# Stick-breaking scores of a hybrid decoder block: three products of rounded and low parts of q and k in place of one plain fp32 product

## The reference

```python
q = rms_norm(heads(sb_q, SB_HEADS), sb_q_norm_g)
k = rms_norm(heads(sb_k, SB_HEADS), sb_k_norm_g)
...
z = jnp.einsum("bhqd,bhkd->bhqk", q_blk, k).astype(jnp.float32) * scale
visible = (kpos[None, :] < t[:, None]) & key_valid[None, :]
log_beta = jax.nn.log_sigmoid(z)
log_one_minus = jnp.where(visible, jax.nn.log_sigmoid(-z), 0.0)
log_remaining = lax.cumsum(log_one_minus, axis=3, reverse=True) - log_one_minus
a = jnp.where(visible, jnp.exp(log_beta + log_remaining), 0.0)
return jnp.einsum("bhqk,bhkd->bhqd", a.astype(v.dtype), v)
```

## Time and profile before

| | |
|---|---|
| three runs, median (lowest to highest) | 1952.8 us (1946.82 to 1953.89) |
| the profiled execution, its own time | 1955.42 us |
| its span, first to last instruction | 1953.6 us |
| mean granted TensorE clock | 0.977 of full |
| TensorE matmul busy | 1859.0 us (95%) |
| VectorE, ScalarE, GpSimd busy | 1392.0, 836.3, 616.0 us |

### The profile page before, as it was taken

How to read it: one execution, slowest core, us unless ns; L and a number is a source line. 1 busy time by engine, 2 the same in 40 slices (tenths; PEclk the granted TensorE clock), 3 DMA queues, 4 the chain that set the end, 5 groups by cost and what they waited for, 6 DMA issues and landing times.

```text
span 1953.6 us, 30169 instructions
## 1 busy us (share of the span) xinstructions
PE 1859.0 (95%) x11211; PEld 1686.9 (86%) x11211; DVE 1392.0 (71%) x2885; ACT 836.3 (43%) x1429; POOL 616.0 (32%) x639
## 2 busy tenths in 40 slices
PE   7899999898986999999999999999999999999999
PEld 7776676666654778899999999999999999999999
DVE  5455455565552654389988869999778888888887
ACT  4335445454453542233434456666433333333332
POOL 4024032041140100059888832121212232223221
PEclk9999989999986999999999999999999999999999
DMA  3220211201203632259999978998889999999996
GB/s 122 99 70 22 71 55 44 82 33 45 87 6 121 199 125 81 84 175 348 334 322 325 326 234 318 336 339 319 282 271 333 336 331 341 333 336 342 331 333 228
DMA packets 150961, 416.12 MB, mean 213 GB/s; under 512 B 16000, under 2 KB 64288, under 8 KB 148768
## 3 DMA queue, kind: packets, MB, share of 16 engines
q1 hardware_dynamic: 110784, 269.31, 38.9%
q0 software_dynamic: 40032, 144.89, 22.7%
HBM read 364.55 MB, written 49.58 MB: 212 GB/s over the span
## 4 chain that ended last, share of the span: by engine, by line
PE 65%; issue 1%; DMA 1%; POOL 1%; DVE 1%; ACT 0%; SPq 0%; DVEq 0%; POOLq 0%; ACTq 0%
PE psE L84 21%; PE psE L86 21%; PE psE L85 21%; PE psE L2093 1%; PE psE L2094 1%; PE psE L2054 1%; DMA gates<-mix_gates 0%; DMA mixer_out<-mixed_heads 0%; POOL few_gathered L1660 0%; POOL expert_lo L1666 0%; DVE few_y L1896 0%; DVE expert_lo L1702 0%; SPq L1514 0%; PE psE L2113 0%; PE psE L2060 0%
## 5 line engine op out<-in xcount | busy, mean ns | idle before, releaser
L84 PE MATMUL psE<-x2h,expert_hi 128*128 128x384 f32 x1024 | 347.3, 339 | 3.8 <-POOL expert_lo L1666 3.8
L84 PE MATMUL psE<-w_hi,expert_hi 128*128 128x384 f32 x1024 | 343.3, 335 | 2.0 <-DVE expert_lo L1702 2.0
L86 PE MATMUL psE<-x2h,expert_lo 128*128 128x384 f32 x1024 | 342.9, 335 | 0.0
L85 PE MATMUL psE<-x2l,expert_hi 128*128 128x384 f32 x1024 | 342.8, 335 | 0.0
L85 PE MATMUL psE<-w_lo,expert_hi 128*128 128x384 f32 x1024 | 342.8, 335 | 0.0
L86 PE MATMUL psE<-w_hi,expert_lo 128*128 128x384 f32 x1024 | 342.7, 335 | 0.0
L1547 ACT ACTIVATE expert_hi<-raw 128x1024 fp32r<-128x1024 f32 x288 | 303.5, 1054 | 63.3 <-PE psE L86 53.6
L1702 DVE TENSOR_TENSOR expert_lo<-raw,expert_hi 128x1024 fp32r<-128x1024 f32 x214 | 261.9, 1225 | 84.7 <-ACT expert_hi L1547 83.1
L1660 POOL DMA_INDIRECT few_gathered<-in_peer_v,picked_expert x128 | 142.3, 1112 | 398.9 <-DVE few_y L1896 356.9
L1666 POOL TENSOR_TENSOR expert_lo<-raw,expert_hi 128x1024 fp32r<-128x1024 f32 x74 | 177.7, 2402 | 161.2 <-ACT expert_hi L1547 159.8
L1601 ACT ACTIVATE w_hi<-gelu 128x384 fp32r<-128x384 f32 x128 | 67.4, 527 | 344.8 <-PE psE L86 342.3
(11 more groups left out here) (339 smaller groups left out, 3518.4 us busy)
## 6 DMA issues: line engine op xcount, KB each, us to landing
raw<-in_peer_u SPq DMA_DIRECT2D x128, 512.0 KB
raw<-in_peer_v SPq DMA_DIRECT2D x128, 512.0 KB
expert_acts<-gelu SPq DMA_DIRECT2D x124, 192.0 KB
gelu<-expert_acts SPq DMA_DIRECT2D x124, 192.0 KB
expert_gates<-shared SPq DMA_DIRECT2D x16, 1024.0 KB, 10.6
gates_in<-expert_gates SPq DMA_DIRECT2D x32, 512.0 KB
ring<-in_w_xonly SPq DMA_DIRECT2D x24, 512.0 KB, 3.3
ring<-in_w_full SPq DMA_DIRECT2D x16, 512.0 KB, 3.8
```

The lines of the kernel that those rows point to most:

```text
L84: nc.tensor.matmul(out, sh, mh, start=first, stop=False)
L85: nc.tensor.matmul(out, sh, ml, start=False, stop=False)
L86: return nc.tensor.matmul(out, sl, mh, start=False, stop=last)
```

## The change

q and k, scaled in place as before by VectorE, are each split: ScalarE copies them to fp32r (the high part of q lies where `exp_g_row` was, that of k in the third row of `conv_act`), and VectorE subtracts that from the fp32 value and writes the low part in place. The copies stand on ScalarE behind the rounding of the next weight chunk (the filler's `kk` place) and the filler place "inverse0", the subtractions on VectorE behind the nine block copies. The score becomes three products, high by high, high of k by low of q, low of k by high of q, summed in PSUM, and the first score of a pair waits for both low parts.

```diff
--- before.py
+++ after.py
@@ -238,8 +238,8 @@
         x, xl = in_place("x", "xl", [P, DC, TOK])
         ring_h = sb("ring_h", [P, FRONT_RING, DC, P], F32R)
         ring, ring_l = in_place("ring", "ring_l", [P, FRONT_RING, DC, P])
-        proj = sb("proj", [P, 4, TOK])
-        qz = sb("qz", [P, 2, SEQ])
+        proj, proj_r = in_place("proj", "proj_low", [P, 4, TOK])
+        qz, qz_r = in_place("qz", "qz_low", [P, 2, SEQ])
         v = sb("v", [P, NT + 1, SEQ])
         ba = sb("ba", [P, NT + 1, 16])
         soft, floor = sb("soft", [P, NT + 1, 16]), sb("floor", [P, NT + 1, 16])
@@ -274,10 +274,12 @@
         soft_h = act_r[:, :, :].rearrange("p w t -> p (w t)")[:, 0:2 * SEQ].rearrange("p (s t) -> p s t", t=SEQ)
         acc_h = kq_r[:, :, :, :].rearrange("p n w t -> p (n w t)")[:, 0:2 * SEQ].rearrange("p (s t) -> p s t", t=SEQ)
         qd = sb("q_decayed", [P, NT + 1, P])
-        egr = sb("exp_g_row", [P, NT + 1, P])
+        egr, egr_r = in_place("exp_g_row", "q_high", [P, NT + 1, P])
         kbg, ktl, vb = (sb(name, [P, NT + 1, P]) for name in ("kbg", "k_tail", "v_beta"))
         rows_all, rows_r = in_place("rows_all", "soft_lo", [P, 2, 2, TOK])
         lows = rows_r[:, :, :, :].rearrange("p k e t -> p (k e t)")[:, 0:4 * SEQ].rearrange("p (s t) -> p s t", t=SEQ)
+        qn_h, qn_l = egr_r[:, :, :].rearrange("p n t -> p (n t)")[:, 0:SEQ], qz_r[:, 0, :]
+        kn_h, kn_l = act_r[:, 2, :], proj_r[:, 0, :]
         soft_l, acc_l = lows[:, 0:2, :], lows[:, 2:4, :]
         row_heads = sb("row_heads", [P, 2, P])
         decays = sb("decays", [P, NT + 1, 2, 2, P])
@@ -303,7 +305,7 @@
             first_level qd_ready level_ready xt_ready x_transposed x_ready y_ready y_copied x_products x_updated wt_ready
             wt_copied v_new_ready v_new_copied o_ready state_product state_ready o_copied o_squared o_sum o_log o_root
             z_ready z_scores z_ln z_soft soft_split later_summed later_high later_ready cumulated att_exp att_out masks_ready
-            att_stored pair_done o_normed o_final state_blank att_inputs state_decayed""".split()
+            att_stored pair_done o_normed o_final state_blank att_scaled att_high att_inputs state_decayed""".split()
         S = {name: sem(name) for name in names}
         x_loaded = [sem(f"x_loaded{k}") for k in range(DC)]
         v_loaded = [sem(f"v_loaded{k}") for k in range(DC)]
@@ -327,7 +329,7 @@
                    wt_copied=1, v_new_ready=5, v_new_copied=5, o_ready=1, state_product=4, state_ready=4, o_copied=1,
                    o_squared=1, o_sum=1, o_log=1, o_root=1, z_ready=1, z_scores=10, z_ln=10, z_soft=10,
                    soft_split=10, later_summed=8, later_high=8, later_ready=8, cumulated=10, att_exp=10, att_out=1, att_stored=1,
-                   o_normed=1, o_final=1, state_blank=1, att_inputs=1, state_decayed=1)
+                   o_normed=1, o_final=1, state_blank=1, att_scaled=2, att_high=2, att_inputs=2, state_decayed=1)
         inc = lambda ins, name, by=1: ins.then_inc(S[name], by)
 
         def waiter(eng, i):
@@ -655,6 +657,11 @@
                         turned = bank[:, y_bank(n), 0:2 * P].rearrange("p (e b c) -> p e b c", e=2, b=2)
                     inc(nc.scalar.activation(into, turned, ACT.Copy), "x_ready")
                 split("inverse0")
+                for part, (high, scaled) in enumerate(((qn_h, qn), (kn_h, kn))):
+                    wait("att_scaled", part + 1)
+                    wait("qd_ready", 1)
+                    wait("transposed", 1)
+                    inc(nc.scalar.activation(high, scaled, ACT.Copy), "att_high")
                 for u, (unit, a) in enumerate(UNITS):
                     if unit == "level":
                         for n in range(NT + 1):
@@ -944,14 +951,18 @@
                                                     xt[0:r, n - 1, :, 0:r], ALU.subtract), "xt_ready")
                 dve.wait_ge(S["w_taken"], CHUNKS.index(("q", i)) + 1)
                 wait("roots", 4)
-                nc.vector.scalar_tensor_tensor(out=qn, in0=qn, scalar=gq, in1=rt[:, 2, META:], op0=ALU.mult,
-                                               op1=ALU.mult)
+                inc(nc.vector.scalar_tensor_tensor(out=qn, in0=qn, scalar=gq, in1=rt[:, 2, META:], op0=ALU.mult,
+                                                   op1=ALU.mult), "att_scaled")
                 inc(nc.vector.scalar_tensor_tensor(out=kn, in0=kn, scalar=gk, in1=rt[:, 3, :], op0=ALU.mult,
-                                                   op1=ALU.mult), "att_inputs")
+                                                   op1=ALU.mult), "att_scaled")
                 for n in range(NT + 1):
                     for rows in halves if n else [slice(0, META)]:
                         last = nc.vector.tensor_copy(mtc[rows, n, :, 0:rows.stop - rows.start], mtat[rows, n, :, 0, rows])
                     inc(last, "blocks_ready")
+                for part, (low, scaled, high) in enumerate(((qn_l, qn, qn_h), (kn_l, kn, kn_h))):
+                    wait("att_scaled", part + 1)
+                    wait("att_high", part + 1)
+                    inc(nc.vector.tensor_tensor(low, scaled, high.bitcast(F32), ALU.subtract), "att_inputs")
                 at("inverse0")
                 for u, (unit, a) in enumerate(UNITS):
                     if unit == "products":
@@ -1225,13 +1236,14 @@
                         r, q0 = tile_rows(kb), first_query(kb)
                         lo, hi = tile_cols(kb)
                         if a == 0:
-                            wait("att_inputs", 1)
+                            wait("att_inputs", 2)
                             if i + 1 < PAIRS:
                                 pe.wait_ge(S["w_taken"], CHUNKS.index(("dq", i + 1)) + 1)
                         if a >= 2:
                             wait("att_exp", a - 1)
-                        last = mm(bank[0:r, a % 2, q0:], kn[half(e), lo:hi], qn[half(e), q0:], start=True, stop=False,
-                                  skip_group_check=True)
+                        for k_part, q_part in ((kn_h, qn_h), (kn_h, qn_l), (kn_l, qn_h)):
+                            last = mm(bank[0:r, a % 2, q0:], k_part[half(e), lo:hi], q_part[half(e), q0:],
+                                      start=k_part is kn_h and q_part is qn_h, stop=False, skip_group_check=True)
                         if kb:
                             if i == 0 and a == 0:
                                 pe.wait_ge(S["masks_ready"], 1)
```

## The result

| | before | changed |
|---|---|---|
| median of five runs each | 1950.2 us | 1963.1 us |
| lowest to highest | 1946.8 to 1953.9 | 1960.0 to 1966.4 |
| profiled execution, own time | 1955.4 | 1962.3 |
| its span | 1953.6 | 1960.2 |

The ratio is 1.0062, 95% interval 1.0044 to 1.0080: slower by 12 us, outside the range of 1941 to 1958. The profiled execution of before is slower than all five runs of the table, so the two traces differ by 6.9 us only, and what they show must be read with that in mind.

What follows compares the result with a forecast made beforehand. TensorE bounds the back part, chains through TensorE, ScalarE and VectorE the front. From 1952.8 us, -11.4 for cheaper scores and +7.2 for the later first score gave 1948.6; own range 1944 to 1954, 8 in 10 runs 1941 to 1958.

Steps and rivals of the forecast that it cites:

- Part 2: Ahead of each pair's first score: it waits for VectorE's subtractions, +1.8 us per pair, +7.2 us in four.
- Part 1: Attention scores: three rounded products replace one plain fp32 product, 2.6 us less per pair, -11.4 us with the clock.
- The step that failed: TensorE around the scores: each switch between plain fp32 and rounded products costs about 0.09 us.
- The other step: Ten scores of a pair: of TensorE's 1.9 us saved per head, 2.6 us per pair reach the end.
- Rival C: Attention stage: clock falls after the new 1.8 us idle, 3.9 us per stretch, four giving 1964.2 us; chance 0.10.
- Rivals A and D: A: TensorE alone limits everywhere, 1943.5 us, chance 0.20. D: attention-stage clock dips fall away, 1940.8 us, chance 0.06.
- B: Front part: the gain drowns in waits on ScalarE and GpSimd, leaving +7.2 us, 1960.0 us; chance 0.08.

Runs made afterwards that it cites:

- experiment 2: Also called products alone: changed kernel with three products of the high parts only, no subtractions, first score waiting only for ScalarE's copies; 1949.2 us, ratio 0.9987.
- wait alone: Also called experiment 1: plain fp32 scores as before, but copies and subtractions are made, unused, and waited for; 1970.8 us, ratio 1.0107 to the kernel before.
- experiments 5 and 6: 5: plain scores, waiting for copies and one 128-column subtraction, 1957.3 us (1.0020). 6: changed kernel, more projection steps planned ahead of the first score, 1945.6 us (0.9963).
- low parts first: Changed kernel with ScalarE's copies ahead of the weight rounding and the subtractions ahead of the block copies; 1948.5 us, ratio 0.9993 to the kernel before.
- the control: The changed kernel as it is, run again beside the kernel before; 1963.4 us, ratio 1.0063.
- the first group: Runs of wait alone, experiment 2, low parts first and the control on one chip, with the kernel before beside them at 1950.8 us.
- experiment 8: Low parts first, with the mask's product ahead of the three score products; 1944.5 us, ratio 0.9955 to the kernel before.

## Why the prediction was wrong

**Part 2, the longer way to the first score, was right in kind and nearly in size**: 8.4 us against 7.2. TensorE's wait on VectorE's low part of k stands where it was said to.

Nearly the whole error in size is the subtraction for k, 0.96 us in place of 0.68 in each pair. The price was read from a row over 16 partitions; over 128 partitions the same operation took 1.26 us for 512 columns in the trace of before and 0.62 for 384, so the row did not bound it.

**Part 1 failed, as a mis-sized term**: -11.4 us were forecast. Measured are 0.5 to 0.8 us per pair, 2 to 3 us in all, by pairs at equal clock; experiment 2 (0 to 5 us) agrees. The step that failed is "each change between the two kinds of product costs about 0.09", which took the change of kind as the only cause. A change from 64 rows to 128 costs the same, and behind a projection product the score still starts 0.09 late, with 0.05 to 0.10 more on its first product. So nothing fell away ahead of the scores (5 x 0.09 in the sum) or around the mask. TensorE saved 0.17 us for 512 columns, 0.16 for the meta tile, 0.12 for 384 and 0.08 for 256, lost 0.05 for 128, and came to 0.48 us per head instead of 1.9. The other step, that two thirds of TensorE's saving reach the end (2.6 of 3.8 us per pair), is not shown wrong: of 0.96 us, 0.5 arrived in pair 2 of the two traces and 0.7 in the pairs at full clock.

**Rival C was what happened, and had 0.10; the forecast put the clock behind the new idle at nothing.** Its price was about right: 3.9 us for 10.2 us at half clock in its stretch (16.53 us at 0.69) are 0.38 per microsecond, near the 0.42. Its trigger was weighed wrongly. I argued against it that the waits of about 1 us in every pair do not always bring a dip. They do not, but an idle of 2 us brought one behind z0 in all twelve pairs that had it (changed kernel twice, wait alone), one of 0.55 to 0.85 in three of seven (experiments 5 and 6), and no pair with z0 on time had one in its first 5 us (before, products alone, low parts first). Four such stretches of 3.4 us at half clock cost 4 x 3.4 x 0.42 = 5.7 us. That C's 1964.2 lies so near to the 1963.1 measured is luck: it kept the full -11.4 of part 1 and took four dips of 3.9 us, 15.6.

**The account.** 8.4 for the wait, about -2 for the products, +5.7 for the clock behind it: +12 us, against 12.6 measured in the control. The clock term is no clean difference of two traces: later dips shift too, and the profiled before was itself one of its slower runs, with dips that the changed kernel lacks (from z9 of the last pair to its end it takes 3.1 us more). The granted clock over all runs of the first group, 0.9802 before and 0.9775 changed, gives an estimate that does not hang on two traces: 2 x 0.0027 x 1957 = 10.6 us more at half clock, 4.4 us at 0.42. For the wait alone (0.9723) it gives 13, and 8.4 + 13 is near the 20 measured. That the terms add up to the medians is thus a fit; that the wait costs more than its own length is shown by experiment 1.

**Rivals A and D** (more gain, 0.26 together) had no part in it. Nor had B: in the whole front TensorE waits 26.4 us for ScalarE (25.9 before) and 1.0 for GpSimd (0.6), and the waits on VectorE grow by the 8.1 us ahead of z0 and little else. The Trainium skill's rule for weight loads ("TensorE: Matmul & The Clock Gate", "LDWEIGHTS (loading the stationary operand)": columns divided by 1.2 in nanoseconds, whatever the rows, so 107 ns) held: the second and third of the 128-column products with k's 64 rows stand 0.11 us apart.

## What to carry to other kernels

Before a cheaper product is paid for with a longer preparation, find the first user of the prepared operand and put the preparation ahead of whatever else its engines have queued: here two subtractions stood behind nine copies that nobody needed as soon, and moving them and ScalarE's copies was worth 15 us (1963.4 to 1948.5). An idle of TensorE had two prices here, its length and the lower clock behind it; put work that is due anyway into it. The price of a product read from a run of like products leaves out what a change of operand kind or of the number of rows costs at each end, which for short products is as large as the saving.

## What was not expected of the hardware

- Behind a product over 64 rows, one over 128 rows starts about 0.09 us late even when both have rounded operands (128-row mask behind 0.11-spaced products: 0.20; behind a 128-row projection product, experiment 8: 0.12).
- Three products of 64 rows over 128 columns (0.47 us up to the mask) take longer than one plain fp32 product (0.42).
- After 2 us of idle the granted clock fell to half for 3.4 to 6.8 us while TensorE was already busy again; not in one pair only, but in all twelve with that wait.
- The nearly full stage from z0 to z9 stretches by only 0.42 us per microsecond at half clock, not by the half microsecond that a TensorE at work all the time would lose.
